# Sample softmax and value products moved into the prompt's attention steps, on one Trainium2 core

## What is computed

```python
def fox_sample(q, k, v, logf, k_past, v_past, logf_past):
    suffix = lax.cumsum(lfp, axis=1, reverse=True) - lfp
    s_past = jnp.einsum('nqhd,nkhd->nhqk', q, k_past).astype(jnp.float32) * scale
    s_past = s_past + cnT[..., None] + suffix.transpose(0, 2, 1)[:, :, None, :]
    s_new = jnp.einsum('nqhd,nkhd->nhqk', q, k).astype(jnp.float32) * scale
    ...
    p = jax.nn.softmax(jnp.concatenate([s_past, s_new], axis=-1), axis=-1).astype(v.dtype)
    o = (jnp.einsum('nhqk,nkhd->nqhd', p[..., :P], v_past)
         + jnp.einsum('nhqk,nkhd->nqhd', p[..., P:], v))
...
    mixed = jnp.concatenate([rmsnorm(y_a, g[:W_A]), rmsnorm(y_b, g[W_A:W_A + W_B]),
                             rmsnorm(y_c, g[W_A + W_B:])], axis=-1)
    x = x + mixed @ lw['w_o']
    x = x + hier_moe(rmsnorm(x, lw['g_ffn']), ...)
```

## Time and profile before

| | us |
|---|---|
| Median of 3 runs (lowest, highest) | 1093.56 (1087.73, 1096.13) |
| The profiled execution | 1092.19 |
| Its span, first to last instruction | 1090.4 |
| PE busy | 886.6 (81%) |
| DVE, ACT, POOL busy | 334.0, 193.2, 264.0 |
| DMA, mean rate over the span | 290 GB/s |

### The profile page before, as it was taken

One profiled execution on the slowest core, in us unless ns is written; L12 is line 12 of the kernel. 1 busy time (PEld: TensorE's weight loads), 2 busy tenths in 40 slices (PEclk: granted clock), 3 DMA queues, 4 the chain that ended last, 5 costly groups with the idle time before them and its releaser, 6 DMA issues.

```text
span 1090.4 us, 11578 instructions
## 1 busy us (share of the span) xinstructions
PE 886.6 (81%) x4285; PEld 465.3 (43%) x4285; DVE 334.0 (31%) x672; ACT 193.2 (18%) x391; POOL 264.0 (24%) x333
## 2 busy tenths in 40 slices
PE   5999689998697779768997787787787887885895
PEld 3888456767543335333333233333333333331342
DVE  4897456464651222460000000000000000000652
ACT  3200234544100000211101101101101101110432
POOL 6889249400012220002111111101111111001110
PEclk9999879999598898888988888988988989998898
DMA  9899526316028986705999999999999999997300
GB/s 310 320 336 372 202 95 232 119 37 243 10 83 328 399 328 238 303 5 181 404 408 415 397 402 410 409 404 413 409 412 414 405 397 413 424 404 297 150 40 38
DMA packets 53799, 316.42 MB, mean 290 GB/s; under 512 B 11214, under 2 KB 24078, under 8 KB 33016
## 3 DMA queue, kind: packets, MB, share of 16 engines
q1 hardware_dynamic: 34704, 233.28, 53.7%
q0 software_dynamic: 14480, 76.17, 18.5%
q10 hardware_dynamic: 4576, 6.46, 1.7%
HBM read 309.31 MB, written 14.82 MB: 297 GB/s over the span
## 4 chain that ended last, share of the span: by engine, by line
PE 48%; DMA 36%; DVE 8%; POOL 2%; issue 2%; ACT 2%; SPq 1%; POOLq 0%; DVEq 0%; ACTq 0%
DMA arena<-in_w_up 29%; PE psum L1611 14%; PE psum L1237 6%; PE psum L1719 5%; PE psum L1313 5%; PE psum L1462 5%; DMA arena<-in_cache_v,indices 4%; PE psum L1383 2%; DMA arena<-in_w_in 1%; DMA arena<-in_w_down 1%; POOL arena L692 1%; DVE arena L1791 1%; PE psum L1567 1%; PE psum L1626 1%; PE psum L1325 1%
## 5 line engine op out<-in xcount | busy, mean ns | idle before, releaser
L1611 PE MATMUL psum<-arena 128*64 128x512 f32 x1024 | 269.6, 686 | 86.4 <-DMA arena<-in_w_up 86.4
L1611 PEld LDWEIGHTS psum<-arena 128*64 128x64 f32 x1024 | 92.2, 157 | 239.7 <-issue 237.6
L2238 DVE TENSOR_TENSOR arena<-arena,psum 64x512 f32<-64x512 f32 x32 | 22.1, 692 | 385.3 <-ACT arena L1095 385.3
L1626 PE MATMUL psum<-arena 128*64 128x512 f32 x512 | 116.0, 592 | 2.1 <-DMA arena<-in_w_down 2.1
L692 POOL TENSOR_TENSOR arena<-arena 128x2048 f32<-128x2048 f32 x20 | 90.6, 4534 | 1.8 <-ACT arena L854 1.4
L1237 PE MATMUL psum<-arena 128*128 128x260 f32 x384 | 85.1, 383 | 0.2 <-DMA arena<-in_w_in 0.2
L746 POOL COPY indices<-row_list 128x1 int32 (+1 forms) x26 | 4.6, 178 | 307.0 <-ACT arena L1101 307.0
L1095 ACT ACTIVATE arena<-psum 64x512 f32<-64x512 f32 x32 | 18.8, 588 | 336.4 <-PE psum L1611 336.4
L1313 PE MATMUL psum<-arena 128*128 128x260 f32 x320 | 78.1, 398 | 0.0
L1237 PEld LDWEIGHTS psum<-arena 128*128 128x128 f32 x384 | 72.6, 190 | 12.3 <-issue 1.3
L1791 DVE TENSOR_REDUCE arena<-arena 128x32 f32<-128x2048 f32 x32 | 72.0, 2281 | 5.8 <-POOL arena L692 5.3
(11 more groups left out here) (320 smaller groups left out, 872.3 us busy)
## 6 DMA issues: line engine op xcount, KB each, us to landing
arena<-in_w_down SPq DMA_DIRECT2D x32, 2048.0 KB, 25.6
arena<-in_w_gate SPq DMA_DIRECT2D x31, 2048.0 KB, 18.3
arena<-in_w_up SPq DMA_DIRECT2D x31, 2048.0 KB, 22.8
arena<-in_w_in SPq DMA_DIRECT2D x11, 1024.0 KB, 6.9
arena<-in_x_prompt SPq DMA_DIRECT2D x8, 512.0 KB, 5.9
arena<-in_w_o SPq DMA_DIRECT2D x1, 4096.0 KB, 14.0
arena<-in_w_ple_gate SPq DMA_DIRECT2D x1, 4096.0 KB, 24.5
arena<-moe_rows SPq DMA_DIRECT2D x4, 1024.0 KB, 7.9
```

Of the source, the lines that this page charges most:

```text
L1611: last = mm(bank(s)[m * SLOTS:(m + 1) * SLOTS, :], hgT[s][:, k, :], w_gu[s][m][:, k, :], start=(k == 0), stop=(k == DC - 1))
L1626: last = mm(bank(6 + s)[n * SLOTS:(n + 1) * SLOTS, :], actT[s][:, k, :], w_dn[s][:, k, n * BANK:(n + 1) * BANK], start=(k == 0), stop=(k = ...
```

## The change

The samples' softmax and value products move into the attention of the prompt, from step 3 on.

- All of the samples' softmax stands at steps 3 to 7 (`sample_max`, `sample_max_all`, `sample_subtract`, `sample_sums_p` on DVE, `sample_max` on PE, the exponents at step 6 on ACT); the sums over the partitions follow the last step. The new row's scores are taken before the first step.
- `values` of chunks 0 to 25 stand at steps 7 and 9 to 15, chunks 26 to 31 in pairs among the norms. `spread_p` stands one step or so ahead of them, and `p_exp` has eight buffers. Chunks 0 to 3 and 4 to 13 add into bank 6, which is also the attention output's, and DVE carries their sums away (`take_values`); chunks 14 to 31 add into bank 7.
- `SHARED` is 28: DVE takes four more chunks in pairs and no longer waits for the prompt's values between the pairs. The reduces of chunks 28 to 31 stand at steps 1 to 3.
- `CK_STEP` and `GV_STEP` put the spreads a little earlier, and `layer_norms` at step 9 where it was at 12.
- The roots of the second norm are two instructions on POOL each.

The diff, cut to its core:

```diff
-SHARED = 24
-V_AFTER = {9: (0, 1), 10: (2, 3)}
-REDUCE_AT = {24: (1, 0), 25: (1, 1), 26: (2, 1), 27: (3, 0), 28: (3, 1), 29: (4, 1), 30: (5, 1), 31: (6, 0)}
+SHARED = 28
+REDUCE_AT = {28: (1, 0), 29: (1, 1), 30: (2, 1), 31: (3, 0)}
...
+VALUES_AT = {7: (0, 1, 2, 3), 9: (4, 5, 6, 7), 10: (8, 9, 10), 11: (11, 12, 13), 12: (14, 15, 16), 13: (17, 18, 19), 14: (20, 21, 22),
+             15: (23, 24, 25)}
...
+VALUE_GROUPS = ((0, 4), (4, 14), (14, 32))
+EXPANDED = 8
...
-CK_STEP = {h: 4 * (h // 2 - 1) + 1 + h % 2 for h in range(2, HC)}
-GV_STEP = {3: 0, 4: 1, 7: 2, 8: 3, 11: 4}
+CK_STEP = {2: 0, 3: 1, 4: 4, 5: 5, 6: 8, 7: 9}
+GV_STEP = {3: 0, 4: 1, 6: 2, 7: 3, 8: 4}
...
+            for t in sorted(TURN, key=TURN.get):
+                w = tile_width(t)
+                r = stats[0:w, 56 + t:57 + t]
+                pool.wait_ge(x1_ms, TURN[t] + 1)
+                step(pool.tensor_scalar(r, stats[0:w, 24 + t:25 + t], 1.0 / D, EPS, ALU.mult, ALU.add))
+                pool.tensor_tensor(r, r, minus_half[0:w, :], ALU.pow).then_inc(x1_root, 1)
...
                 if c:
                     pe.wait_ge(a_of, c)
+                    pe.wait_ge(pv_read, min(c, 2))
...
                 if s:
                     transpose_p(s - 1)
+                for n in VALUES_AT.get(s, ()):
+                    values(n)
...
             norm_sums("normC")
+            values_left(2)
...
             norm_sums("normA")
             norm_sums("normB")
-            wait_free(pe, "newT")
-            pe.wait_ge(new_ready, 1)
-            done(tr(fill("newT")[0:NB, 0:HC], new_s[0:NB, :], ident[0:NB, 0:NB]), "newT")
+            values_left(len(left))
...
-            mix_out(0, (0, 1, 2))
-            softmax_T("maxT", 1, slice(0, HC), max_p)
...
-            values_step(0, first=True)
-            mix_out(1, (1,))
-            values_step(1)
-            mix_out(1, (2, 3))
-            values_step(2)
+            mix_out(0)
+            mix_out(1)
             route(0)
-            for m in range(4):
-                values_step(3 + m)
-                mix_out(2, (m,))
+            mix_out(2)
             route(1)
-            values_step(7, last_one=True)
...
             for s in range(STEPS):
                 negate_scores(s)
+                if s == 5:
+                    sample_max_all()
+                if s == 6:
+                    sample_subtract()
+                if s == 7:
+                    sample_sums_p()
+                if s == 8:
+                    take_values(0)
+                if s == 12:
+                    take_values(1)
+                for n in SPREAD_AT.get(s, ()):
+                    spread_p(n)
...
-                dve.wait_ge(x1_ms, TURN[t] + 1)
-                root(stats[0:w, 56:57], stats[0:w, 24 + t:25 + t], 1.0 / D)
+                dve.wait_ge(x1_root, TURN[t] + 1)
```

More of the change, by code:

```diff
@@ L1415, in spread_norm, with values_left @@
                 done(last, name)
+            left = list(range(max(VALUES_AT[max(VALUES_AT)]) + 1, CHUNKS))
+            def values_left(n):
+                for _ in range(n):
+                    values(left.pop(0))
+            wait_free(pe, "sum")
+            pe.wait_ge(smp_req, 3)
+            done(mm(fill("sum")[0:NB, 0:HC], col_sel, sum_p, start=True, stop=True), "sum")
             wait_free(pe, "state")
@@ L1942, in _ @@
                     layer_norms()
+            for n in range(max(SPREAD_AT[max(SPREAD_AT)]) + 1, CHUNKS):
+                spread_p(n)
+            wait_full(dve, "sum")
+            dve.wait_ge(smp_p, 2)
+            step(v.tensor_tensor(sum_s[0:NB, :], fill("sum")[0:NB, 0:HC], pnew[0:NB, :], ALU.add))
+            dve.nop().then_inc(free_of("sum"), 1)
+            step(v.reciprocal(sum_s[0:NB, :], sum_s[0:NB, :]))
             dve.wait_ge(half_free, rest_halves - 4)
```

233 lines of the change are left out of this document (126 added, 107 removed).

## The result

The changed kernel takes 1080.32 us, the median of six runs (1077.75 to 1082.52), where the kernel before took 1094.42 in the same rounds (1087.73 to 1096.13). The ratio is 0.988, with an interval of 0.9855 to 0.9905: faster by 1.2%. The forecast of 1063 is missed, and so is the range, by 1.3 us at its upper end. The direction is right. By the medians 14.1 us of the expected 29.1 came.

The account below looks back on a forecast made before the run. The change moves PE work from a stage bound by gathers into the attention, bound by PE. Terms -4.5 - 1.3 + 30.0 + 4.7 - 56.9 - 1.1 = -29.1 from 1092.19 give 1063 us; range 1046 to 1079.

Parts of the forecast that it names:

- Part 1: Ahead of the first `diagonal`: DVE goes on with keys instead of idling, so the attention starts earlier; gain 4.5 us.
- Part 2: Attention steps 0 to 4: old DVE waits go, `sample_max` and the spread of head 4 cost some; gain 1.3 us.
- Part 3: Attention steps 5 to 16: 26 value chunks at 1.07 us and new waits of 5.2 us on PE; loss 30.0 us.
- under 2 us: Sign that the forecast holds: waits for gathers in the attention come to less than this in all.
- four rivals: Late gathers, 1078 (0.17); no waits, 1054 (0.10); attention at lower clock, slower (0.04); gain not reaching the end, 1090 (0.03).
- Part 4: Norms behind the attention: three blocks of two chunks in PE's chain, 6.4 us, less 1.7 of DVE's work; loss 4.7 us.
- Part 5: Output projection, emptied of value chunks: 56.8 us where 113.7 were; gain 56.9 us.
- Part 6: Second norm's roots on POOL instead of DVE: 1.1 us more from the samples' tile; gain 1.1 us.
- signs of being wrong: Waits for gathers in most steps, a clock under 0.9 in the attention, or a stage behind 411 that grows.

Follow-up runs that it names:

- e4: Kernel before, with only the new rows' three score instructions moved to where POOL runs two products back to back: 1100.9 us, ratio 1.0071.
- e1: Changed kernel, with the three instructions of the new rows' scores moved into `sample_max` at step 3: 1067.9 us, ratio 0.9758.
- e2: Changed kernel, with the 8x8 subtraction replaced in place by a multiplication with a constant (one input, forget gates left out): 1077.8 us, ratio 0.9851.
- e3: Changed kernel, with POOL's second product of the last four made to wait for the first `diagonal`: 1069.5 us, ratio 0.9765.
- e5: Changed kernel, score instructions in place, but the sums go to PSUM and the 8x8 subtraction reads them there: 1068.9 us, ratio 0.9774.
- e13: Changed kernel with new scores by way of PSUM, layer norms dealt out over steps 9 to 13, gating tiles 0 and 1 at steps 2 and 3: 1056.0 us.
- e7: e1 with the layer norms dealt out, one tile a step over steps 9 to 13: 1060.8 us, ratio 0.9703.
- e6: e1 with the second norm's roots back on DVE instead of POOL: 1071.4 us, ratio 0.9798.

## Why the prediction missed

**Part 1, the attention starts earlier: wrong, and the main miss (13.6 us of 19.4).** DVE's key work was right to 1 us: by the sum its reduces end at 134.2, and they ended at 134.99. The step that failed is "a product and a reduce over 512 columns, each like such a copy, and a small one: 1.7". It took 14.3, because the small one stood still beside POOL's three products. The product and the reduce cost 0.69 and 0.67, as priced; the product was done 0.2 us before POOL began, which is luck, since in e4 it was the product that stood still. The small one was priced without a row and without a look at its neighbour: by the prediction's own plan POOL's products run there, and the subtraction has its inputs and its output in SBUF. Shown by e1, e2, e3 and e5, and by e4 in the other kernel. A gain of 4.5 became a loss of 9.1.

The Trainium skill (SBUF — State Buffer, SBUF: two separate sides) says that VectorE and GpSimd share a pair of ports under an exclusive lock, taken by a VectorE instruction with two SBUF inputs (against a GpSimd one that reads SBUF) or in a mode that uses both ports. The waits of the changed kernel and of e4, and their absence in e5, agree. The Trainium skill (VectorE: DVE Perf Modes, What auto-detection actually checks) gives that mode to a single source and a destination that are both in SBUF, with outermost sizes both even or equal. The 8x8 multiplication of e2 meets this, and its 12.92 us agree; that section does not say whether RECIPROCAL, which took 0.16, can have the mode. The lock is said to last for the whole instruction. Here the runs show more: the subtraction was kept waiting over three products in a row, 12.92 us where the rest of the first was 4.0.

**Part 2, steps 0 to 4: 4.2 us too low.** From the first `diagonal` to step 5 it took 45.4 us, not 41.2. The step that failed is the count of bank 7's users at step 4. The prediction let the spread of head 4 wait 1.8 us for DVE (it waited 0.74), and left out that gating tile 1 uses the same bank in the same step, behind ACT's copy and DVE's `diagonal`: 2.98 us at 190.20, and behind it a `weigh_values` of 4.54 us, where the sum had 2.4. e13 shows it (4 us, with the new scores out of step 3).

**Part 3, steps 5 to 16: 113.7 us, 2.4 too low; its terms were off with opposite signs.** The chunks cost 24.6 us (24.63 busy for 416 records), not 27.8: 1.07 holds for the first of a block, each further one takes 0.87. The trace of the kernel before had it already:

```profile
346.42 3.66 PE L1383 MATMUL psum<-arena 128*32 128x256 f32 x64
```

PE's waits came to 8.8 us (113.7 less 104.87 busy), where the sum had 5.2. The wait for the layer norms was predicted at its place and nearly at its size, 3.2 against 3.84; those at steps 7 and 15 did not come, and in their place gathers cost 2.5 and the second double use of bank 7, at step 8, 1.64. And a wait was taken to cost only itself. Behind the one of 3.84 the four products of `query_keys` take 2.08 us, 1.13 at full clock, and the `rest_step` 4.52, where the others take 3.77: 1.7 us more; in e1 the same wait cost 7.1 us in all, by e7. The prediction bounded the clock's answer between waits of 2.2 and 0.74 us and gave it nothing in this stage. The rule of the Trainium skill that it weighed (TensorE: Matmul & The Clock Gate, HAM oscillation) has bursts of work fall back to the lower clock again and again when waits stand between them. In this stage the trace does not agree: the mean clock is 0.97, and it fell behind one wait.

**Gathers:** 2.5 us in all, "under 2 us" was nearly right. None of the four rivals is what happened: the gathers were on time, waits were there, the clock held in the attention, and what was gained reached the end.

**Part 4, the norms: loss 6.0, predicted 4.7.** The term that was off is the six chunks' 6.4 us. They took 9.0: the first and the last block of two ran at the lower clock (3.47 and 3.64 us), the middle one at full (1.93). The window's mean clock, 0.71 instead of 0.62, and waits shorter by 1.1 us gave some of it back.

**Part 5, the output projection: gain 60.0, predicted 56.9.** Four terms were each a little too dear. The way from tile 2 to the samples' output took 6.3 us, not 7.4: its root was taken with 1.1 us less, and e6 shows 2.3, because it overlaps a wait. The first two tiles with their slow start took 29.9 and not 30.9, `route` 0 took 3.7 and not 4.3, and the third tile 13.8 and not 14.1.

**Part 6, the roots: right in size at its place, 1.3 us for 1.1.** In the changed kernel it doesn't show, since the stage behind the samples' output is 85.4 us long where 84.4 were, one of the prediction's own signs of being wrong. PE was busy 0.7 us longer for the same 272 records. Where these 2.1 us come from was not settled.

**Step by step in sum:** 13.6 + 4.2 + 2.4 + 1.3 - 3.1 + 2.1 (behind the samples' output) = 20.5, less 0.4 in the experts' stage and 0.7 behind it: 19.4. What was gained ahead of the experts reached the end. With the repair of part 1 alone the kernel runs at 1067.9 to 1068.9, inside the range, but not for the sum's own reasons throughout: parts 2 to 4 and the stage behind the samples' output were too low by 10.0, and part 5, too high by 3.1, took some of it back.

## What to carry to other kernels

Before a VectorE instruction is moved, look at what GpSimd does at its new place: for an instruction with both inputs in SBUF, and for the multiplication with a constant from SBUF to SBUF, the price beside long GpSimd products without a gap was the rest of their run, however small the instruction. Route one operand through PSUM, or move it to where GpSimd has a gap. Count who else uses a bank in the step that a spread is moved into. And price a wait of TensorE of about 4 us with what the clock takes behind it: here such a wait cost nearly twice itself.

## What the runs showed of the hardware

- An 8x8 VectorE instruction took 12.92 us beside three GpSimd products, 4.03 when a gap followed the first, 0.15 with one input in PSUM, and 0.15 where GpSimd ran no product but a series of 0.2 us instructions with gaps (e1). An 8x512 product took 6.90 instead of 0.69. VectorE's reduces, its 128x1 RECIPROCAL and the instructions with a PSUM input that stood there ran beside the products at their usual price, and GpSimd's products took 4.5 us each all the same.
- It seems to go the other way too: a gather's issue on GpSimd took 1.80 us instead of 0.94 where VectorE had just begun a 128x1024 instruction with two inputs in SBUF (180.11 against 179.89 in the changed kernel, and so in its variants). No run varied it, so this is an observation without a tested cause.
- Blocks of 16, 32, 48 and 64 records of `values` took 1.07, 1.93, 2.80 and 3.66 us at full clock: 0.87 for each further chunk, 0.2 more for the first.
- A wait of 3.91 us for PE brought the four products behind it from 1.13 to 2.08 us, and PE's busy time in that stage from 106.4 to 109.5 us (e7 and e1).
